# GpSimd makes the low part of every second weight block, from the query tiles of the second layer to the read-out's projection

## The reference

```
o, _, _ = hgrn_bidir(q_prep(p_q), to_heads(p_i), hgrn_forget(p_ff, lb_f), hgrn_forget(p_fb, lb_b), s_f, s_b)
y_h = hgrn_readout(o, p_g, hgrn_norm_g, hgrn_out_w)      # norm, gate, projection
y_c = conformer_branch(p_cv, p_cg, ..., conv_pw_w, rows)
y   = (sigmoid(p_gc) * y_c + sigmoid(p_gh) * y_h) @ w_out
x   = x + ga_m * rms_norm(y, norm_post_mix)
x   = x + ga_f * rms_norm(square(relu(h2 @ mlp_w1)) @ mlp_w2, norm_post_mlp)
```

## Time and profile before

| | us |
|---|---|
| Median of 3 runs | 2089.68 |
| Lowest, highest run | 2088.97, 2091.5 |
| Profiled execution, its own time: first to last instruction (the span) | 2089.8 |
| TensorE busy (matmul) | 2052.2 (98%) |
| VectorE busy | 1568.9 (75%) |
| ScalarE busy | 1035.9 (50%) |
| GpSimd busy | 81.4 (4%) |
| Moved by DMA | 449.87 MB, mean 215 GB/s |

### The profile page before, as it was taken

How to read it: one execution, slowest core, us unless ns; L and a number is a source line. 1 busy time by engine, 2 the same in 40 slices (tenths; PEclk the granted TensorE clock), 3 DMA queues, 4 the chain that set the end, 5 groups by cost and what they waited for, 6 DMA issues and landing times.

```text
span 2089.8 us, 31175 instructions
## 1 busy us (share of the span) xinstructions
PE 2052.2 (98%) x12480; PEld 1804.9 (86%) x12480; DVE 1568.9 (75%) x2370; ACT 1035.9 (50%) x1560; POOL 81.4 (4%) x73
## 2 busy tenths in 40 slices
PE   8999999999999999999999999999999999999997
PEld 8999999888888888998888888788888888888886
DVE  6889986779798686678879898576766756656665
ACT  6876445656423223545555555555445435434543
POOL 0000020110000000000000001200000000000012
PEclk9999999999999999999999999999999999999999
DMA  7778897667524666444438989555875766555552
GB/s 289 233 245 288 299 319 261 235 197 256 162 99 158 206 236 228 140 143 131 141 131 311 336 289 343 164 173 193 275 239 190 258 215 197 181 190 195 188 178 98
DMA packets 122690, 449.87 MB, mean 215 GB/s; under 512 B 13745, under 2 KB 14129, under 8 KB 122033
## 3 DMA queue, kind: packets, MB, share of 16 engines
q1 hardware_dynamic: 122544, 447.88, 63.2%
HBM read 443.63 MB, written 4.19 MB: 214 GB/s over the span
## 4 chain that ended last, share of the span: by engine, by line
PE 72%; DVE 2%; ACT 1%; issue 0%; POOL 0%; POOLq 0%; ACTq 0%; DVEq 0%
PE bank L859 72%; DVE WL L1558 0%; DVE AR L1565 0%; PE bank L1017 0%; DVE SR L1565 0%; ACT WH L1157 0%; DVE AR L1558 0%; ACT AR L1157 0%; ACT AR L1158 0%; ACT L1158 0%; POOL AR L2165 0%; PE bank L1048 0%; ACT SR L1158 0%; POOL AR L2167 0%; DVE AR L1661 0%
## 5 line engine op out<-in xcount | busy, mean ns | idle before, releaser
L859 PE MATMUL bank<-SR,WH 128*128 128x512 f32 (+1 forms) x6240 | 1715.1, 361 | 15.9 <-DVE WL L1558 7.6
L859 PE MATMUL bank<-SR,WL 128*128 128x256 f32 (+1 forms) x4960 | 1124.7, 285 | 1.6 <-DVE SR L1565 1.6
L859 PEld LDWEIGHTS bank<-SR,WL 128*128 128x128 f32 x4960 | 936.8, 189 | 168.5 <-DVE SR L1565 3.0
L859 PEld LDWEIGHTS bank<-SR,WH 128*128 128x128 f32 x6240 | 986.5, 190 | 64.6 <-issue 18.4
L1157 ACT ACTIVATE WH<-WF 128x1024 fp32r<-128x1024 f32 x636 | 671.5, 1057 | 483.7 <-PE bank L859 431.0
L1558 DVE TENSOR_TENSOR WL<-WF,WH 128x1024 fp32r<-128x1024 f32 x636 | 770.2, 1223 | 127.0 <-ACT WH L1157 123.1
L1157 ACT ACTIVATE AR<-bank 128x256 f32<-128x256 f32 (+1 forms) x262 | 107.1, 413 | 312.8 <-PE bank L859 309.5
L1565 DVE SCALAR_TENSOR_TENSOR AR<-WF,SM,AR 128x512 f32<-128x512 f32 (+1 forms) x210 | 208.2, 1017 | 4.6 <-DMA WF<-in_mod 0.2
L1558 DVE TENSOR_TENSOR AR<-AR 128x256 f32<-128x256 f32 (+3 forms) x366 | 149.3, 438 | 48.7 <-ACT AR L1158 33.2
L1558 DVE TENSOR_TENSOR AR<-bank,AR 128x256 f32<-128x256 f32 (+1 forms) x234 | 100.3, 431 | 99.0 <-ACT AR L1157 68.9
L2160 POOL TENSOR_TENSOR AR<-AR 128x256 f32<-128x256 f32 x56 | 68.1, 1216 | 1990.8 <-ACT AR L1158 1990.7
(11 more groups left out here) (90 smaller groups left out, 546.6 us busy)
## 6 DMA issues: line engine op xcount, KB each, us to landing
WF<-in_mlp SPq DMA_DIRECT2D x256, 512.0 KB, 4.0
WF<-in_mod SPq DMA_DIRECT2D x192, 512.0 KB, 5.1
WF<-in_w_in SPq DMA_DIRECT2D x176, 512.0 KB, 4.3
WF<-in_a_in SPq DMA_DIRECT2D x64, 512.0 KB, 5.2
WF<-in_a_out SPq DMA_DIRECT2D x32, 512.0 KB, 6.1
WF<-in_ple_g SPq DMA_DIRECT2D x32, 512.0 KB, 4.6
WF<-in_w_out SPq DMA_DIRECT2D x32, 512.0 KB, 5.9
WF<-in_pw SPq DMA_DIRECT2D x16, 512.0 KB, 3.4
```

Source lines behind the costliest of these rows:

```text
L859: return tensor.matmul(o, l, r, start=start, stop=stop, skip_group_check=True)
```

## The change

Which engine makes a block's low part is written into the block when the timetable is made. For the tiles named in `SHARED` (query and read-out gate, pointwise projection, convolution merge gate, read-out projection) blocks with an odd running number among the weight blocks go to GpSimd, the others stay with VectorE. GpSimd has its own `low_part`, the same subtraction of the same shape, and its own semaphore `w_lp`; TensorE's wait and the release of the WF slot look up which semaphore and which count belong to the block. GpSimd's program is now a walk over the step list as well; its other work keeps its order and its waits.

```diff
--- before.py
+++ after.py
@@ -61,6 +61,8 @@
 PAIRED = tuple(range(8, 20)) + (22, 23)
 
 COPIED = {"pleg": 0, "cv": 15 - 40, "cg": 23, "q": 31, "pw": 39, "gc": 55, "hout": 71, "gh": 87, "wout": 103}
+
+SHARED = {"w_in": ((24, 40), (56, 72)), "pw": ((0, 16),), "hout": ((0, 16),)}
 
 XPIECES = [(0, 2), (2, 4), (4, 8), (8, 12), (12, 16)]
 
@@ -178,10 +180,15 @@
 
 
 
-    count = {"w": 0, "v": 0, "p": 0}
+    count = {"w": 0, "v": 0, "p": 0, "vector": 0, "pool": 0}
     for b in blocks:
         count[b["of"]] += 1
         b["n"] = count[b["of"]]
+        if b["of"] == "w":
+            shared = any(lo <= b["index"] < hi for lo, hi in SHARED.get(b["name"], ()))
+            b["low"] = "pool" if shared and b["n"] % 2 else "vector"
+            count[b["low"]] += 1
+            b["low_n"] = count[b["low"]]
 
     tile, uses = {}, [0] * 8
     closes, rows_at = [], []
@@ -618,7 +625,7 @@
         sem(n) for n in ("s_gain", "s_par", "s_mk", "s_p", "s_c", "s_keep", "s_back", "s_out"))
     s_x = [sem(f"s_x{q}") for q in range(len(XPIECES))]
 
-    w_hi, w_lo, prod, mod_v, mod_p = (sem(n) for n in ("w_hi", "w_lo", "prod", "mod_v", "mod_p"))
+    w_hi, w_lo, w_lp, prod, mod_v, mod_p = (sem(n) for n in ("w_hi", "w_lo", "w_lp", "prod", "mod_v", "mod_p"))
     free = [sem(f"free{g}") for g in range(GBANKS)]
     close_t, row_a, row_t, row_v = (sem(n) for n in ("close_t", "row_a", "row_t", "row_v"))
 
@@ -767,9 +774,16 @@
 
         return sg_v, n + 1
 
+    weights = [b for b in blocks if b["of"] == "w"]
+
+    def low_done(k):
+
+        b = weights[k]
+        return (w_lp if b["low"] == "pool" else w_lo), b["low_n"]
+
     def freed(i):
         b = blocks[i]
-        return {"w": w_lo, "v": mod_v, "p": mod_p}[b["of"]], b["n"]
+        return low_done(b["n"] - 1) if b["of"] == "w" else ({"v": mod_v, "p": mod_p}[b["of"]], b["n"])
 
     def mod_blocks(cg):
 
@@ -874,7 +888,7 @@
             if part == "high":
                 w.wait_ge(w_hi, n + 1)
             else:
-                w.wait_ge(w_lo, n + 1)
+                w.wait_ge(*low_done(n))
             if start:
                 g, uses, _ = tile[(kind, j)]
                 w.wait_ge(free[g], uses - 1)
@@ -2071,7 +2085,7 @@
 
         running = {}
         for what, *a in steps:
-            if what == "low":
+            if what == "low" and blocks[a[0]]["low"] == "vector":
                 low_part(*a)
             elif what == "modv":
                 mod_sum(a[0])
@@ -2143,28 +2157,46 @@
 
     def pool_program(pool):
         w = Once(pool)
+        def low_part(i, k):
+            w.wait_ge(w_hi, k + 1)
+            pool.tensor_tensor(WL[:, k % NB, :], WF[:, i % NF, :], raw(WH[:, k % NB, :]), ALU.subtract).then_inc(w_lp, 1)
+
+        def add_square(group, ft):
+            if 0 < ft < 15:
+                w.wait_ge(sq, 16 * group + ft + 1)
+                w.wait_ge(acc, 14 * group + ft - 1)
+                pool.tensor_tensor(ACC, ACC, SQ[ft % 2], ALU.add).then_inc(acc, 1)
+
         pool.memset(ONES[:, :], 1.0).then_inc(ones_ok, 1)
-        for group in range(4):
-            if group == 3:
+        shares = [(at, width) for at, width, by in LAST if by == "p"]
+        for what, *a in steps:
+            if what == "low" and blocks[a[0]]["low"] == "pool":
+                low_part(*a)
+            elif what == "evac" and a[0][0] == "aout":
+                add_square(0, a[0][1])
+            elif what == "after" and a[0] == "pleg" and a[2] == 3:
+                add_square(1, a[1])
+            elif (what == "after" and a[0] == "wout" and a[2] == 2) and ("wout", a[1]) not in WHOLE:
+                add_square(2, a[1])
+            elif what == "add_y2" and a[0] == 0:
                 w.wait_ge(st_cp, 1)
                 w.wait_ge(*left(("wout", 15)))
                 w.wait_ge(s_back, 16)
-                for n, (at, width) in enumerate((at, width) for at, width, by in LAST if by == "p"):
+                for n, (at, width) in enumerate(shares):
                     y = YO1[:, at:at + width, :]
                     pool.tensor_tensor(y, y, rs_b(RSTD[0], width), ALU.mult).then_inc(p_own, 1)
                     w.wait_ge(p_own, n + 1)
                     pool.tensor_tensor(XT2[:, at:at + width, :], XT2[:, at:at + width, :], y, ALU.add).then_inc(x3_p, 1)
-            for ft in range(1, 15):
-                w.wait_ge(sq, 16 * group + ft + 1)
-                w.wait_ge(acc, 14 * group + ft - 1)
-                pool.tensor_tensor(ACC, ACC, SQ[ft % 2], ALU.add).then_inc(acc, 1)
-        w.wait_ge(y2_s, 1)
-        w.wait_ge(st_cp, 2)
-        for n, (at, width) in enumerate((at, width) for at, width, by in LAST if by == "p"):
-            y = YO2[:, at:at + width, :]
-            pool.tensor_tensor(y, y, rs_b(RSTD[0], width), ALU.mult).then_inc(p_own, 1)
-            w.wait_ge(p_own, sum(by == "p" for *_, by in LAST) + n + 1)
-            pool.tensor_tensor(y, y, XT2[:, at:at + width, :], ALU.add).then_inc(out_p, 1)
+            elif what == "evac" and a[0][0] == "mlp2" and a[0][1][0] == 3:
+                add_square(3, a[0][1][1])
+            elif what == "finish":
+                w.wait_ge(y2_s, 1)
+                w.wait_ge(st_cp, 2)
+                for n, (at, width) in enumerate(shares):
+                    y = YO2[:, at:at + width, :]
+                    pool.tensor_tensor(y, y, rs_b(RSTD[0], width), ALU.mult).then_inc(p_own, 1)
+                    w.wait_ge(p_own, len(shares) + n + 1)
+                    pool.tensor_tensor(y, y, XT2[:, at:at + width, :], ALU.add).then_inc(out_p, 1)
 
     blk = ctx.enter_context(nc.Block())
     blk.sync(sync_program)
```

## The result

The changed kernel takes 2112.03 us (median of 4 runs, 2109.05 to 2118.52) against 2090.43 (2088.97 to 2091.5): 1.0109 of the time before, 95% interval 1.0097 to 1.0121. It is 21.6 us slower. The forecast was no difference, 2090 us, and its range ended at 2100. The profiled execution took 2113.26 us, its span 2111.4 against 2089.8, so the two traces show the same 21.6 us.

The account below looks back on a forecast made before the run. TensorE, busy 98% of the span, was taken as the bound, with 4.6 us of waits to win. Terms of -1.4, +1.5 and 0 summed to +0.1 on 2089.8 us: 2090 us, no difference, range 2086 to 2100.

Parts of the forecast that it names:

- rival 3: GpSimd's fp32r form is dear, 4.7 us per low part: 2117 us; chance 0.05.
- The ceiling of the gain: TensorE's waits between 872 and 1100 us, 4.6 us together, are the most that the change can win.
- The one wait that was walked through: TensorE's 1.7 us wait before a recurrence product at 949.72 us: 0.4 us gained, leaving 1.3.
- term 3: Read-out projection: 8 holds covered by PSUM evictions and slack, so 0; ends 0 and +2.6 us.
- the waits of rows 3: TensorE's six profiled waits between 872 and 1100 us in the kernel before, 4.6 us together.
- term 1: TensorE's waits between 872 and 1100 us shrink through VectorE's relief: -1.4 us; ends 0 and -4.6.
- three level stretches: Seven-level recurrence stretches of three head pairs, such as 949.7 to 974.0 us, with VectorE busy 23.1 of 24.3.
- term 2: Seven-level recurrence stretches: holds outweigh savings, +0.5 us each, +1.5 for three; ends 0 and +7.3.
- The forecast's own bound: Prediction called wrong if TensorE's waits from 872 to 1100 us leave 2 to 9 us.
- Where VectorE's queue is full, it tends to win: At 308.44 us two VectorE low parts passed GpSimd's earlier add (3.42 us), so holds fall on gaps, not the chain.
- Rival 1: Hold becomes the bound in three level stretches and the read-out projection, nearly 2.2 us each: +10, 2100 us; chance 0.30.

Follow-up runs that it names:

- the tail: Changed kernel with sharing only in the last three query tiles and first two read-out gate tiles, 5 low parts moved: 2096.04 us, 1.0027.
- the head: Changed kernel with sharing only in the first five query tiles, 5 low parts moved: 2092.13 us, 1.0006.
- The four pieces: Changed kernel with each GpSimd subtraction cut into four instructions of 256 columns: 2101.39 us, 1.0053.
- the run with the fills: Changed kernel, but GpSimd subtracts only 16 columns per block, after zero-filling the other 1008 twice: 2085.95 us, 0.998.

## Why the prediction was wrong

**What held.** GpSimd's price: 2.41 us (median) against 2.36 predicted, and the fp32r form costs nothing more, which ends rival 3. The two engines do exclude each other when VectorE reads two SBUF operands. A full hold takes 2.1 to 2.2 us from VectorE and a moved low part gives 1.0 to 1.14 back. Lateness costs nothing. The ceiling of the gain, 4.6 us, was of the right size (3.5 measured). The one wait that was walked through, before 949.7 us, is 1.34 us long where 1.3 was forecast. The read-out projection takes its 8 holds at nothing when it is changed alone, as term 3 had it; in the full change its stage is 2.0 us longer, 1.5 of it in a wait for a GpSimd low part, inside the end of +2.6.

**The terms, one by one.** The two traces have the same 12480 matmuls in the same order, so the delay of each can be read off, and with it what each part of the changed stages lost:

| Part | forecast, us | measured, us |
|---|---|---|
| query tiles | no term | +6.3 |
| the waits of rows 3 (term 1) | -1.4 | +4.8 |
| three level stretches (term 2) | +1.5 | +3.2 |
| the rest of the convolution merge gate | no term | +6.0 |
| read-out projection (term 3) | 0 | +2.0 |

**The step that failed most: places without a term.** The query tiles and what lies between and behind the level stretches make 12.3 of the 22.3 us, and the sum had them at nothing. The section on the profile took 35.6 of 52.9 us as VectorE's share of the query tiles, and the working went on with terms for the recurrence only. The mean hid 30 us in which VectorE is 90% busy, and these come first. The holds there met TensorE before the idle time came, most of all the last two: with only the low parts of the tail moved the kernel lost 5.6 us, with only those of the head 1.2, which isn't clear of nothing. In the merge gate it is VectorE's own low part at 1120.06 us, in a stretch where rows 2 gave only a mean as well: a wait of 2.68 us, and the low clock behind it.

**Term 1 had the wrong sign.** I walked through one wait, and it came out. Its relief (-1.14) stands against a hold that lay mostly under a reciprocal, and the trace does show the reciprocal unheld. The other waits were counted after it without a walk. In the kernel before they were 0.28, 0.61 and 0.52 us (at 881.71, 1001.08 and 1053.73 us); in the changed one they are 2.44, 2.67 and 1.46, because there a hold fell on the short operand that TensorE stands for. Between 879.2 and 1116.8 us, where the same matmuls run as from 872 to 1100 in rows 3, TensorE waits for 5.5 + 4.7 + 2.3 = 12.5 us where it waited for 4.6. The forecast's own bound was 9.

**Term 2 was too small, inside its own ends.** The level stretches grew by 1.4, 1.8 and 0.0 us against the +0.5 each; the upper end was +7.3 for all three. So the part that the prediction worked on most is not where it went wrong.

**What is common to them.** The prediction added up saving, hold and idle time over a stretch of 12 or 24 us. A hold comes at once: 2.1 us in one short instruction, against a slack of 0.5 us before the use at 1103.92 us. The overrun is TensorE's loss then and there, and a low part that VectorE is spared a few microseconds later comes too late for it. A low part that it was spared earlier does help, as before 949.7 us and in the query tiles' head. The four pieces fit this, with VectorE relieved on the whole and 11 us lost all the same, but they don't prove it, since the holds together fell too.

**Who wins the port.** "Where VectorE's queue is full, it tends to win" rested on one row, 308.44 us. In the changed kernel 26 of 48 GpSimd low parts weren't held at all, 17 took 2.45 to 3.1 us, no more than the rest of one VectorE instruction longer, and only 5 took over that. The forecast had a median near 3 us; it is 2.41. What the Trainium skill states ("SBUF — State Buffer", Who interferes with whom), that whoever issues first has the shared ports for its whole instruction, fits the pairs at 850.29 and 1120.02 us. One low part, of 4.82 us at 959.79, shows that a GpSimd instruction can still be passed over more than once. The same section of the Trainium skill says that an instruction of VectorE with two SBUF inputs is kept out by a GpSimd instruction that reads SBUF, and not by one that only writes it; the run with the fills agrees: no operation with two inputs was stretched beside them.

**Rival 1 was the case**, with a chance of 0.30 and a price of +10 where +21.6 was measured. Its mechanism is what the runs show. Its place was too small: it had the level stretches and the read-out projection, and left out the query tiles and what lies between and behind the level stretches of the merge gate. Its price also took TensorE's waits alone, and not the 6.1 us in which TensorE is busy for longer, 3.2 of it at the lower clock (848.6 to 852.0 and 1125.1 to 1128.5 us), in matmuls of 0.80 us instead of 0.40.

## What to carry to other kernels

Work given to a second engine isn't free when the two share a way into memory: price it by how long it keeps the first engine out, here up to 2.2 us, 1.4 in the mean, for each 1.0 to 1.1 us saved, and not by how idle the second engine is. Compare that hold, as one lump, with the slack of the tightest place that it can fall on; a stage's mean and a sum over a stretch hide both. An engine that isn't on the critical path gives little when it is relieved, and a lot is lost when it is held: 48 reliefs were worth 3.5 us, and the holds of the 48 low parts cost over 20. And look at which block the helper works on: here it shut VectorE out for a low part that was needed later than the one it delayed.

## What the runs showed of the hardware

- A tensor-scalar operation of 128x512 f32 with one SBUF operand is held too: 2.63 us at 841.77 instead of 0.42 beside a subtraction of GpSimd, and 1.13 us at 839.57 beside a mere fill. Reciprocals (1.75 us), predicated copies with a PSUM operand and tensor-tensor operations with a PSUM operand are not.
- GpSimd's fill of 128x1008 f32 takes 0.947 us and lies beside two-operand VectorE work without holding it; the only operations that the 96 fills stretched were two tensor-scalar ones, by 1.5 us together.
- GpSimd's subtraction into fp32r takes 0.22 us for 16 columns, 0.72 for 256 (the shortest of the 192 pieces) and 2.36 to 2.41 for 1024 where nothing holds it. An f32 operation of 256 columns takes 0.74, so the rounding costs nothing.
- Two waits of TensorE of 1.36 and 2.51 us, 4 us apart, were followed by a granted clock of 0.50 (1.2 GHz) from 852.2 to 855.6 us. A wait of 2.68 us up to 1123.52 us was followed by 0.50 from 1125.1 to 1128.5, and one of 2.55 us up to 849.05 had it from 848.6 to 852.0. The waits of 2.44 and 2.67 us up to 891.12 and 1013.59 us were not followed by it.
